# Attention inside a hybrid decoder layer: order of the key blocks, the place of a group's first transposition, and the engine that makes the query's low parts

## The reference, cut to what matters

```
scale = 1.0 / math.sqrt(dq)                      # dq = 192: 128 without rotation, 64 with
def one_block(args):                             # one block of 128 queries of each head
    qb, start = args
    s = jnp.einsum("bhqd,bhkd->bhqk", qb, k).astype(jnp.float32) * scale
    q_pos = start + jnp.arange(Q_BLOCK)
    mask = key_pos[None, :] <= q_pos[:, None]
    p = jax.nn.softmax(jnp.where(mask, s, -jnp.inf), axis=-1)
    return jnp.einsum("bhqk,bhkd->bhqd", p.astype(v.dtype), v)
```

## Time and profile before

| | us |
|---|---|
| median of three runs | 2991.56 |
| lowest and highest | 2991.54, 2992.53 |
| span of the profiled execution | 2990.1 |
| what lies around the span, against the median | 1.5 |
| TensorE busy over the span | 2817.9 (94%) |
| VectorE, ScalarE, GpSimd busy | 1814.3, 1181.2, 1144.1 |
| attention, first value product to last transposition | 1046.5 to 1410.5, 364.0 |

### The profile page before, as it was taken

How to read it: one execution, slowest core, us unless ns; L and a number is a source line. 1 busy time by engine, 2 the same in 40 slices (tenths; PEclk the granted TensorE clock), 3 DMA queues, 4 the chain that set the end, 5 groups by cost and what they waited for, 6 DMA issues and landing times. The chain is left out here.

```text
span 2990.1 us, 48834 instructions
## 1 busy us (share of the span) xinstructions
PE 2817.9 (94%) x18995; PEld 2440.4 (82%) x18995; DVE 1814.3 (61%) x2759; ACT 1181.2 (40%) x2210; POOL 1144.1 (38%) x1213
## 2 busy tenths in 40 slices
PE   7998979997999899998999599999999999999999
PEld 7997779996888688887788478888788888788887
DVE  3226834443555587777796677777887777543544
ACT  3226722223545365555443433333433333332321
POOL 2535930004776200001553456666666666100000
PEclk9999989997999899999999799999999999999999
DMA  8975953225454022221575633333533333654554
GB/s 269 354 251 171 263 166 111 67 74 130 108 147 87 22 75 91 85 68 40 179 246 164 216 93 105 95 103 94 190 105 99 101 105 97 240 170 146 192 167 142
DMA packets 403278, 421.07 MB, mean 141 GB/s; under 512 B 34075, under 2 KB 325995, under 8 KB 401000
## 3 DMA queue, kind: packets, MB, share of 16 engines
q1 hardware_dynamic: 368400, 298.61, 33.5%
q10 hardware_dynamic: 19944, 66.63, 6.8%
q0 software_dynamic: 14704, 52.69, 5.4%
HBM read 257.51 MB, written 160.34 MB: 140 GB/s over the span
## 5 line engine op out<-in xcount | busy, mean ns | idle before, releaser
L3526 PE MATMUL fu_pM<-fu_us_hi,fu_w_ring 128*128 128x512 f32 x2464 | 772.6, 393 | 15.2 <-DVE fu_us_lo L3361 14.3
L3526 PEld LDWEIGHTS fu_pM<-fu_us_hi,fu_w_ring 128*128 128x128 f32 x2464 | 466.3, 189 | 120.5 <-DVE fu_us_lo L3361 17.0
L3526 PE MATMUL fu_pM<-fu_us_lo,fu_w_ring 128*128 128x512 f32 x1232 | 482.8, 392 | 0.0
L3526 PEld LDWEIGHTS fu_pM<-fu_us_lo,fu_w_ring 128*128 128x128 f32 x1232 | 233.4, 189 | 47.8
L3262 ACT ACTIVATE fu_w_ring<-fu_sw 128x512 fp32r<-128x512 f32 x176 | 110.9, 631 | 325.3 <-PE fu_pM L3526 264.1
L3368 DVE TENSOR_TENSOR fu_w_ring<-fu_sw,fu_w_ring 128x512 fp32r<-128x512 f32 x132 | 139.4, 1056 | 65.4 <-ACT fu_w_ring L3262 65.3
L3368 DVE TENSOR_TENSOR fu_w_ring<-fu_w_raw,fu_w_ring 128x512 fp32r<-128x512 f32 x88 | 108.5, 1233 | 104.3 <-ACT fu_w_ring L3262 104.3
L2995 PE MATMUL fu_pM<-fu_us_hi,fu_w_ring 128*128 128x512 f32 x666 | 169.3, 391 | 1.3 <-DVE fu_w_ring L2918 1.3
L3262 ACT ACTIVATE fu_w_ring<-fu_w_raw 128x512 fp32r<-128x512 f32 x132 | 83.0, 629 | 191.3 <-PE fu_pM L3526 169.9
L3409 DVE SCALAR_TENSOR_TENSOR fu_acc<-fu_gb,fu_taps,fu_acc 128x1024 f32<-128x1024 f32 x88 | 133.0, 1513 | 37.7 <-ACT fu_acc L3303 36.9
L2075 ACT ACTIVATE at_pt_hi<-at_pT 128x512 fp32r<-128x512 f32 (+3 forms) x176 | 92.7, 539 | 143.6 <-PE at_pT L2340 142.7
(11 more groups left out here) (539 smaller groups left out, 7141.5 us busy)
## 6 DMA issues: line engine op xcount, KB each, us to landing
fu_w_ring<-scr_gs ACTq DMA_DIRECT2D x37, 704.0 KB, 4.6
fu_w_raw<-in_w_gate SPq DMA_DIRECT2D x22, 1024.0 KB, 5.4
fu_w_raw<-in_w_up SPq DMA_DIRECT2D x22, 1024.0 KB, 5.4
scr_gs<-fu_sg SPq DMA_DIRECT2D x84, 256.0 KB, 3.0
scr_gs<-fu_acc SPq DMA_DIRECT2D x63, 256.0 KB, 2.9
fu_us_lo<-scr_gs ACTq DMA_DIRECT2D x19, 704.0 KB, 4.6
pj_wd<-in_w_down POOLq DMA_DIRECT2D x11, 1024.0 KB, 9.3
scr_td<-pj_td POOLq DMA_DIRECT2D x11, 1024.0 KB, 8.0
```

The lines of the kernel that those rows point to most:

```text
L3526: p = pe.matmul(bank(2 * n + m, i)[:, :], a[:, k, :], x[:, k, :], start=(k == 0 and n_pass == 0), stop=(k == HALVES_K - 1 and n_pass == 2))
```

## The change

1. The key blocks of a group come in the order meta, the four diagonal blocks, then the full blocks from the first on. Step m keeps its place in all counters; `block_of(n, m)` says which block it is, and `first_tile` takes its width from there.
2. TensorE issues `turn(n + 1, 0)` behind the value products of the last step of group n instead of ahead of them. Its four transpositions wait row by row for the exponentials. The programs of ScalarE and VectorE are not changed for this.
3. For groups 2 to 15 the low parts of the queries are made on GpSimd, not on VectorE. On GpSimd the split of group n+3 stands behind the store of group n's output. TensorE's first score of a group waits for GpSimd's semaphore there.

```diff
+        KEY_BLOCKS = [[0] + list(range(QB * g + 1, QB * g + QB + 1)) + list(range(1, QB * g + 1)) for g in range(GROUPS)]
+        def block_of(n, m):
+            return KEY_BLOCKS[ORDER[n][1]][m]
-        def first_tile(m):
-            return max(m - 1, 0)
+        def first_tile(n, m):
+            return max(block_of(n, m) - QB * ORDER[n][1] - 1, 0)
...
+            def split_q(n):                                   # gpsimd
+                s = n % 2
+                pool.wait_ge(q_half, n + 1)
+                pool.tensor_tensor(q_lo[s][:, :], f(q_lo[s][:, :]), f(q_hi[s][:, :]), ALU.subtract)
+                pool.tensor_tensor(qr_lo[s][:, :], f(qr_lo[s][:, :]), f(qr_hi[s][:, :]), ALU.subtract).then_inc(q_ready_late, 1)
...
+            split_q(2)
             for n, (h, g) in enumerate(ORDER):
                 at = N_META + GW * g
                 pool.wait_ge(o_done, n + 1)
                 pool.dma_start(S["o_mla"][at:at + GW, h * VD:h * VD + VD].rearrange("(i p) d -> p i d", p=P),
                                o_sb[n % 2][:, :, :]).then_inc(stored[n % 2], 16)
+                if n + 3 < NG:
+                    split_q(n + 3)
...
-                    if m == 1 and n + 2 < NG:                 # vector
-                        split_q(n + 2)
...
                 if k == 0:                                    # tensor, scores
-                    pe.wait_ge(q_ready, n + 1)
+                    if n < 2:
+                        pe.wait_ge(q_ready, n + 1)
+                    else:
+                        pe.wait_ge(q_ready_late, n - 1)
...
-                    if m == 0:                                # tensor, turn
-                        pe.wait_ge(p_ready, QB * (n + 1))
-                    at = N_META + P * (m - 1) if m else 0
-                    for i in range(first_tile(m - QB * ORDER[n][1]), QB):
+                    key = block_of(n, m)
+                    at = N_META + P * (key - 1) if key else 0
+                    for i in range(first_tile(n, m), QB):
+                        if m == 0:
+                            pe.wait_ge(p_ready, QB * n + i + 1)
                         t = pe.transpose(pT[x % NPT][:, i, :], rows[n % 2][i][:, at:at + P], ident[:, :])
...
-                    if m == QB * g + 1:                       # tensor, values
+                    if m == 1:
                         pe.wait_ge(kv_split, split_count(h, "v", g))
-                    v_hi, v_lo = v[h % 2][:, m - 1, 0, :], v[h % 2][:, m - 1, 1, :]
+                    key = block_of(n, m)
+                    v_hi, v_lo = v[h % 2][:, key - 1, 0, :], v[h % 2][:, key - 1, 1, :]
...
                     for tn, tm in turns(n, m):
-                        turn(tn, tm)
+                        if tm != 0:
+                            turn(tn, tm)
                     for k in issued(n, m):
                         scores(n + 1, k)
                     values(n, m)
+                    if m == STEPS[n] - 1 and n + 1 < NG:
+                        turn(n + 1, 0)
```

More of the change, by code:

```diff
@@ L1922, in stage_attention @@
         loaded = S["at_loaded"]
-        q_loaded, q_half, q_ready = S["at_q_loaded"], r.sem("q_half"), r.sem("q_ready")
+        q_loaded, q_half, q_ready, q_ready_late = S["at_q_loaded"], r.sem("q_half"), r.sem("q_ready"), r.sem("q_ready_late")
         kv_half, kv_split = r.sem("kv_half"), r.sem("kv_split")
@@ L2070, in hi @@
             def hi(n, m):
-                x, at = SB[n] + m, P * first_tile(m - QB * ORDER[n][1])
+                x, at = SB[n] + m, P * first_tile(n, m)
                 act.wait_ge(t_done, TURN[n, m] + 1)
@@ L2348, in values @@
                 h, g = ORDER[n]
-                x, at = SB[n] + m, P * first_tile(m - QB * g)
+                x, at = SB[n] + m, P * first_tile(n, m)
                 pe.wait_ge(t_used, x + 1)
```

## The result

The changed kernel is slower: 3002.68 us (median of 10 runs, 2998.37 to 3004.52) against 2992.05 (10 runs beside it), a ratio of 1.0034 with an interval of 1.0025 to 1.0043, or 7.5 to 13 us. The forecast was 2990.0 in a range of 2983 to 2996, with 0.12 on slower.

A forecast was written before the change was run, and what follows sets the result against it. TensorE, busy 343.7 of the attention's 364.0 us, was taken to set the time. Terms at the group ends, g = 3 and group 15 summed to -1.6 us, taking the median from 2991.56 to 2990.0, range 2983 to 2996.

The forecast's parts named there:

- signs of being wrong: Profile after: wrong if TensorE's wait for L2209 doesn't grow, or if VectorE's splits are longer than 0.7 us.
- the sum changes only through waits: Group ends, g = 1 to 3: reordering moves 1.52 us of TensorE's work from end to start, none of it gone.
- g = 0 ends, a gain of 0.64 each: Four g = 0 to 1 boundaries: last products and three transpositions done during the last exponential; gain 0.64 us, 0.39 to 0.75.
- none at the end of a g = 3 group: End of g = 3 groups in the kernel before: TensorE not idle, since the successor's rows are short.
- g = 2, a loss of 0.03 each: Four g = 2 to 3 boundaries: last products wait on exponential, high part, low part; next turn at 1295.2 against 1295.16.
- g = 1, -0.36 to +0.33: Four g = 1 to 2 boundaries: gain 0.36 us in head 0, 0.06 in two heads, loss 0.33 in head 3.
- g = 3, "I take 1.4 between the ends 1.2 and 2.0": Steps 1 to 8, paced by VectorE: 1.4 us won, against 1.52 more TensorE work later; loss 0.1 each, three groups.
- Group 15, 0.7: Last group, no query split: reciprocal begins 0.8 us earlier, 1.52 stands behind it; loss 0.7 us, 0.2 to 1.5.
- The row-wise waits, 0: Three added waits in each of 15 first turns: 0 to 3.6 us in all, taken as 0.
- Rival 2: g = 3 groups: GpSimd's pair stretches VectorE's subtractions from 0.68 to 1.79 us, first scores late; 2999 to 3005, chance 0.12.

The follow-up runs named there:

- place-alone run: Kernel before with only the first turn moved behind the last products, one wait for all four transpositions, old key order, query low parts on VectorE: 3000.74 us, 1.0031.
- order alone: Kernel before with only the new key block order, first turn at its old place, query low parts on VectorE: 2993.78 us, 1.0006.
- order and turn: Kernel before with the new key order and the moved first turn with row-wise waits, query low parts on VectorE: 3003.94 us, 1.0032.

## Why the prediction was wrong

It had the mechanism of a group's end right, most small terms too low by some tenths, one term wrong by much, and one place not looked at. One of its own signs of being wrong came true: VectorE's splits were to be no longer than 0.7 us, and five were 1.62 to 1.94. By its own steps:

- *"the sum changes only through waits", and the wait for the exponential is replaced by one for the last step's products*: right. L2209's successor grew, L2340's shrank.
- *g = 0 ends, a gain of 0.64 each*: right at the spot (0.75 to 0.17 behind the release, and 0.67 where this edit stood with GpSimd's). It was lost again elsewhere: **moving a first turn behind the last products** was priced only at the boundary where it gains. At g = 3 ends, whose exponential is long done, the last products no longer stand between the turn and the first products of the next group, which need its high and low part: 0.3 us each, in the place-alone run too. I had written these ends off with "none at the end of a g = 3 group", which counts the idle time there and not what the turn covered.
- *g = 2, a loss of 0.03 each*: 0.41. H, the start of the last high part, came 1.18 earlier against the group's first turn (1299.04 - 1269.32 against 1294.14 - 1263.24), not 1.40; products and turn took 1.24 (1300.41 to 1301.65), not 1.08. Two errors of 0.2 in one direction, where the terms themselves were that small. (The forecast's own terms, not rounded on the way, give a gain of 0.02 and not a loss of 0.03; it makes no difference.)
- *g = 1, -0.36 to +0.33*: 0.14 to 0.46. Place alone costs 0.43 at each; the order gives some 0.2 back in two of the four heads. The forecast saw that ScalarE stays the bound, but not that the old place had the turn's 0.39 lie under the low part's 1.3 for nothing.
- *g = 3, "I take 1.4 between the ends 1.2 and 2.0"*, a loss of 0.1: 1.77. This is the step that failed, 5.0 of the 11.5 us between forecast and profile. The pace in steps 1 to 8 brought 0.1, not 1.4: of the 1.37 that GpSimd took from VectorE, 1.26 came back in the stretched key split. But the turn took more of it than GpSimd did: up to the products of step 8 a group is 0.80 shorter in order alone, 0.31 in order and turn, 0.11 in the changed kernel. And the wide steps at the end cost 1.9 (10.35 us from the products of step 8 to the next group's turn of key step 1, against 8.44), not 1.52; in order alone they cost 1.6.
- *Group 15, 0.7*: 0.79, right.
- *The row-wise waits, 0*: right at the ends (g = 2 and 3 within 0.04). Wrong at the start of the attention, which the forecast never looked at, since its first turn isn't moved: 3.4 us more at the lower level of the clock, 1.6 us net.
- *Rival 2, GpSimd against VectorE, 0.12*: its mechanism happened at the price given (1.94 for the rule's 1.79), but once a group and without late first scores. It is a small part of the loss through what it took from the g = 3 term (0.2 us a group against order and turn), not the loss. In the old order GpSimd's part of the change is no loss (0.9995).
- *The clock*: no term, no rival. The earlier trace rows has 1.00 for the attention, and the forecast put idle stretches of 1.3 to 1.8 us at eight ends of groups without asking what the clock would do behind them. In the changed kernel's own profile it did nothing there; in those of five parts of the change it fell once or twice.

So the time is outside of the range because costs of 0.3 to 0.4 us of one edit, at 11 of the 15 boundaries where it moves a turn, were each set at about zero, and because in g = 3 a gain in VectorE's pace was counted that the moved turn and GpSimd's collision took back.

## What to carry to other kernels

Price a moved instruction at every boundary where it moves, not where it is meant to help; where it had filled the latency of a chain (transposition, high part, low part, product), it leaves that latency bare. Work taken off an engine is only worth what its neighbour doesn't take back: look which of its remaining instructions get longer beside the new owner's (here the splits with both inputs in SBUF), and which of them run at that moment. And if the busiest engine must wait 1.5 us anyway, try some useless work in the wait, but no more than fits: the 24 transpositions at the start held up the first scores by 1.1 and 1.2 us in two of three profiles.

## What the runs showed of the hardware

- Behind idle stretches of TensorE of 1.7 to 2.1 us the granted clock sometimes went from the upper to the lower level for about 3.4 us (0.59 and 0.56 in two windows of 2 us above), at a cost of 1.6 us; at others of 1.7 to 2.0 it didn't, at the same place of the same group size. With transpositions in the wait it stayed at 1.00 behind every group's end in the five profiles that had them.
- At the start of the attention the granted clock stayed at the lower level for 10.2 us in six profiles of kernels whose first turn waits row by row, and for 6.8 or 6.9 in eight with one wait.
- VectorE's subtraction of 128x512 from two SBUF inputs took up to 1.94 us beside GpSimd's and 0.68 alone; that with one input in PSUM took 0.68 beside it.
- GpSimd's subtraction of 128x512 took 1.28 to 1.31 us in 28 of 28 cases of the changed kernel, also beside the stretched splits; in the kernel that holds it back, nine of 28 took 1.41 to 1.75.
